# The last, half-filled chunk of four FFN down products: three full-height matmuls per output become one full-height and one half-height

## The reference, cut to what matters

```
def swiglu(h, w1, w3, w2):
    return (jax.nn.silu(h @ w1) * (h @ w3)) @ w2      # D_MODEL = 1024, D_FF = 2752, SEQ = 256

x = x + 0.5 * m[:, 0, 2][:, None] * swiglu(adaln_in(x, norm_g[l, 0], m, 0), ...)
```

## Time and profile before

| | |
|---|---|
| median of 3 executions | 1446.82 us |
| the profiled execution's own time | 1446.1 us |
| its span | 1444.3 us |
| PE busy | 1373.6 us, 95% of the span, 10822 matmuls |
| PE weight loads busy | 1309.9 us, 91% |
| DVE busy | 1088.4 us, 75% |
| ACT busy | 692.9 us, 48% |
| mean granted TensorE clock | 0.99 |

### The profile page before, as it was taken

The page is one execution under the profiler, slowest core; times in us unless marked ns, Lnnn a source line. Parts: engine busy times, 40 slices in busy tenths (PEclk is TensorE's granted clock), DMA queues, the critical chain, the costliest instruction groups (busy, mean ns, idle before and its releaser), DMA issues.

```text
span 1444.3 us, 26188 instructions
## 1 busy us (share of the span) xinstructions
PE 1373.6 (95%) x10822; PEld 1309.9 (91%) x10822; DVE 1088.4 (75%) x1832; ACT 692.9 (48%) x1121; POOL 24.9 (2%) x24
## 2 busy tenths in 40 slices
PE   2899999899999999999998999999999899999998
PEld 2899998789999989999997799999997678899998
DVE  6788998887787789788678766565676766677766
ACT  3343435554433363334464444344476866555453
POOL 0000000000000000001000000000010120000000
PEclk9999999999999999999999999999999999999999
DMA  9897758246868576584643145655422314154451
GB/s 392 345 403 310 312 198 315 95 189 261 309 263 319 207 284 267 215 346 192 250 184 124 59 175 205 230 199 214 175 89 102 117 62 185 64 201 175 179 192 69
DMA packets 32182, 305.80 MB, mean 212 GB/s; under 512 B 3480, under 2 KB 5784, under 8 KB 7360
## 3 DMA queue, kind: packets, MB, share of 16 engines
q1 hardware_dynamic: 32064, 304.13, 54.5%
HBM read 303.05 MB, written 1.06 MB: 211 GB/s over the span
## 4 chain that ended last, share of the span: by engine, by line
PE 83%; DVE 8%; DMA 4%; ACT 3%; issue 2%; SPq 0%; DVEq 0%; ACTq 0%
PE bank L692 13%; PE bank L696 13%; PE bank L693 13%; PE bank L867 12%; PE bank L786 7%; PE bank L784 7%; PE bank L791 6%; DMA ring<-in_stream 3%; PE bank L661 2%; DVE WL L1842 2%; PE bank L710 1%; DMA PR<-in_stream 1%; ACT WH L1285 1%; PE bank L768 1%; PE bank L960 1%
## 5 line engine op out<-in xcount | busy, mean ns | idle before, releaser
L1842 DVE TENSOR_TENSOR WL<-ring,WH 128x1024 fp32r<-128x1024 f32 x414 | 495.9, 1222 | 56.1 <-ACT WH L1285 54.0
L1285 ACT ACTIVATE WH<-ring 128x1024 fp32r<-128x1024 f32 x414 | 424.6, 1054 | 152.2 <-DMA ring<-in_stream 57.7
L692 PE MATMUL bank<-XH,WH 128*128 128x256 f32 x1648 | 403.0, 283 | 4.1 <-ACT WH L1285 4.1
L693 PE MATMUL bank<-XL,WH 128*128 128x256 f32 x1648 | 401.1, 282 | 0.0
L692 PEld LDWEIGHTS bank<-XH,WH 128*128 128x128 f32 x1648 | 311.1, 189 | 10.2 <-issue 9.0
L693 PEld LDWEIGHTS bank<-XL,WH 128*128 128x128 f32 x1648 | 311.2, 189 | 0.5 <-issue 0.5
L696 PE MATMUL bank<-XH,WL 128*128 128x256 f32 x1648 | 229.4, 282 | 0.0
L696 PEld LDWEIGHTS bank<-XH,WL 128*128 128x128 f32 x1648 | 209.9, 188 | 0.1
L784 PE MATMUL bank<-GH,WH 128*128 128x256 f32 x840 | 202.6, 279 | 0.1
L786 PE MATMUL bank<-GL,WH 128*128 128x256 f32 x840 | 202.5, 279 | 0.0
L1368 ACT ACTIVATE SG<-bank 128x256 f32<-128x256 f32 x84 | 32.2, 384 | 333.9 <-PE bank L696 328.9
(11 more groups left out here) (315 smaller groups left out, 1575.6 us busy)
## 6 DMA issues: line engine op xcount, KB each, us to landing
ring<-in_stream SPq DMA_DIRECT2D x128, 1536.0 KB, 6.6
scr<-in_stream SPq DMA_DIRECT2D x15, 1536.0 KB, 10.8
PR<-in_stream SPq DMA_DIRECT2D x15, 1536.0 KB, 9.5
att<-in_stream SPq DMA_DIRECT2D x15, 1536.0 KB, 10.3
ring<-in_stream SPq DMA_DIRECT2D x13, 1024.0 KB, 4.9
ring<-in_stream SPq DMA_DIRECT2D x10, 512.0 KB, 3.7
kf_mix<-in_stream SPq DMA_DIRECT2D x2, 1536.0 KB, 17.0
con<-in_consts SPq DMA_DIRECT2D x1, 1680.0 KB, 14.7
```

The source lines that it names most:

```text
L692: pe.matmul(o, part(WH, u, k), XH[:, k, :], start=(k == 0), stop=False)
L693: pe.matmul(o, part(WH, u, k), XL[:, k, :], start=False, stop=False)
L1285: act.activation(part_all(WH, u), raw(u), ACT.Copy).then_inc(*mark("high", u))
L1842: dve.tensor_tensor(part_all(WL, u), raw(u), part_all(WH, u).bitcast(F32), ALU.subtract)\
```

## The change

For the half chunk, three things differ. (1) VectorE writes the low part of the w2 unit not into WL but over the zero rows 0..63 of its WH slot. (2) VectorE makes a second copy of the rounded G32, into rows 0..63 of GH. (3) TensorE makes, per output m, one product of the full height, which now holds WH·GH in its lower 64 rows and WL·GH in its upper 64 rows, and one product of rows 64..127 alone, WH·GL. The left-over L763 of chunk 20 stays as it is.

```
                             if m == KD - 1:
                                 before.then_inc(*mark("ffn_down", f, c - 1))
-                            for w, x in ((WH, GH), (WH, GL), (WL, GH)):
-                                last = pe.matmul(out(m), part(w, u, m), x[:, c % 2, :], start=False, stop=(w is WL),
-                                                 skip_group_check=True)
-                            last.then_inc(*mark("ffn_out", f, m))
+                            pe.matmul(out(m), part(WH, u, m), GH[:, c % 2, :], start=False, stop=False, skip_group_check=True)
+                            pe.matmul(out(m), part(WH, u, m)[64:P], GL[64:P, c % 2, :], start=False, stop=True,
+                                      skip_group_check=True).then_inc(*mark("ffn_out", f, m))
...
                         dve.wait_ge(*at("high", u))
-                        dve.tensor_tensor(part_all(WL, u), raw(u), part_all(WH, u).bitcast(F32), ALU.subtract)\
-                            .then_inc(*mark("low_dve", u))
+                        name = UNITS[u][0]
+                        if name[0] == "w2" and half_chunk(name[1], name[2]):
+                            low, h = part_all(WH, u)[0:64], slice(64, P)
+                        else:
+                            low, h = part_all(WL, u), slice(0, P)
+                        dve.tensor_tensor(low, raw(u)[h], part_all(WH, u)[h].bitcast(F32), ALU.subtract).then_inc(*mark("low_dve", u))
...
                     if c >= 2:
                         dve.wait_ge(*at("ffn_down", f, c - 2))
+                    if half_chunk(f, c):
+                        dve.tensor_copy(GH[0:64, c % 2, :], G32[h])
                     link(dve.tensor_copy(GH[h, c % 2, :], G32[h]))
```

## The result

The changed kernel takes 1477.83 us (median of 4 runs, 1476.96 to 1479.05); the kernel before takes 1447.95 us (4 runs). The ratio is 1.0211, 95% interval [1.0197, 1.0226]. The forecast was 1459.1 us, with a range up to 1463.5: right about slower, wrong about how much. The profiled execution took 1477.21 us with a span of 1475.3, 31.0 us over the span before.

The account below looks back on a forecast made before the run. TensorE was taken to bound the kernel, VectorE arriving last at all four FFN ends. Per FFN -0.94 + 3.15 + 0.30, written +9.9 in all on 1446.8 us, plus 2.4 for the clock: 1459.1 us, range 1453.5 to 1463.5.

Parts of the forecast that it names:

- What bounds the kernel: TensorE's time counts in full at the FFN ends, VectorE arrives last at all four; DMA is 4% of the path.
- The product that goes: At each FFN end, 24 matmuls in place of 32: 0.94 us less on TensorE.
- The changes of form: Switching between full-height and 64-row products, 16 times per FFN end: 0.19 to 0.20 us each, 3.15 us per FFN.
- Rival (b): At the FFN ends, switching between full-height and 64-row fp32r products into one bank costs nothing: 1444.2 us; chance 0.06.
- (c): Rival: at the FFN ends only one switching direction costs, or half of each, 1.6 us per FFN: 1450.7 us; chance 0.06.
- VectorE's copy: Second copy into GH, on the chain TensorE waits for at all four FFN ends: 0.30 us each, 1.2 in all.
- The low part's new place: VectorE's low part of the w2 unit, 64 rows in place of 128: no change in time, cost 0.
- The clock: TensorE's clock falls to 1.2 GHz once behind each of the first two FFN ends: 1.2 us each, 2.4 together.
- The bounds: For the whole kernel's time, a range of 1453.5 to 1463.5 us around the forecast of 1459.1.
- a fall at all four ends: Rival: TensorE's clock falls in full behind all four FFN ends, 4 x 1.75 us: 1463.7 us; four or more, chance 0.08.
- one to three falls: The forecast's own case, TensorE's clock falling at one to three FFN ends: 1457.9 to 1461.5 us; chance 0.58.

Follow-up runs that it names:

- e1: Changed kernel with the GL product at full height again, GpSimd zeroing GL rows 0..63, no half-height product: 1448.71 us, ratio 0.9993 to the kernel before.
- e3: Kernel before, still three products for the half chunk, but WH x GL made of rows 64..127 alone and no second copy: 1469.74 us.
- e9: Changed kernel with TensorE's wait for VectorE ahead of the four tails filled by 18, 15, 10 and 4 unused full-height products: 1468.83 us.
- e5: Changed kernel with two full products and then two half products per pair of outputs, 8 changes of form per FFN end: 1461.36 us.
- e11: Kernel before with 55 unused full-height products behind each of the four tails, no change of form: 1474.20 us, ratio 1.0195.
- e6: Changed kernel with two unused full-height products per output between the full and the half product: 1479.36 us.
- e2: Kernel before with only VectorE's second copy into GH added: 1450.94 us, ratio 1.0021.
- e4: Changed kernel with the eight half products behind the sixteen full ones, two changes of form per FFN end: 1450.58 us.
- e10: Changed kernel with two unused full-height products per output, and TensorE's wait for VectorE ahead of each tail filled too: 1467.58 us.

## Why the prediction was wrong, step by step

- **What bounds the kernel: right.** VectorE is last ahead of every tail, PE's time in the tail arrives in full at the end of the sums, and no DMA took anything up.
- **The product that goes, 0.94 us: right** (e1: 3.85 to 2.80 to 2.91).
- **The changes of form: right.** I read 0.19 to 0.20 each off and took 3.15 us per end; e3 measured 3.00 and 3.04 with nothing else changed. In the changed kernel the tail at the high clock is 5.86 to 5.94 (e9), 6.0 forecast. Rival (b), that fp32r into one bank would escape it, is out, and so is (c), which had 1.6 us per FFN for the sixteen where e3 has 3.0. Each change costs the same within the error: eight cost half of sixteen (e5, 4.35 - 2.91 = 1.44).
- **VectorE's copy: right, 0.28. The low part's new place: wrong.** I had it at nothing, since its duration would stay 1.22. It did, but in this place VectorE's instructions started 0.08 to 0.09 ahead of the end of the one before, and on either side of the new one they start 0.03 to 0.04 behind it (rows below). That is 0.25 us where VectorE sets PE's start: the two together 2.0 us in place of 1.2.
- **The clock: the step that failed.** I wrote that it would fall "once behind each of the first two, and not behind the other two", for 1.2 us each, 2.4 in all. It fell at all four ends, for 10.2, 10.2, 6.7 and 6.7 us. The ends and the sums grew by 23.8 us; at the high clock they would have grown by 4 x ((5.90 + 3.56) - 7.30) = 8.6 us, so that the clock took 15.2 there, where I had 2.4. Elsewhere the changed kernel's profile has 5.2 us more at the low clock, of which the 4.6 of the third layer are mostly not the change's (e11). Three things were wrong. I read the length of a low stretch off the one window of the earlier trace rows and priced it at 3.5 us. The trace behind that window, the line below, has a mean of 0.55, which is (1 - 0.55) / 0.50 x 3.5 = 3.15 us more, and the earlier trace rows shows the slow products in it. So even that stretch lasted about 6.8 us and was worth up to 3.4, not 1.75. Next, among changes of form it can last longer still: 13.7 us in e6 and e3, against 3.5 in e2. And I thought that the wait ahead was needed, which e9 and the fourth end deny. What was measured without the clock's term is 8.6 + 2.0 = 10.6 us, where my sum had 9.9.

```profile
792.00:795.50 3.50, 3.50 (x20) 3.44 (x19) 2.92 (x9) 2.44 (x10) 0.00 (x0) 0.55 0.00 0
```

- **The bounds.** I priced a fall at all four ends at 4 x 1.75 and gave it 0.08. The range ended at 1463.5 since I had no row of a low stretch inside a tail with changes of form, and put the end at the nearest one instead of asking how long it could last. Four falls of 3.4 us would have been 13.6, and 1470.3. The upper bound of 1461.5 for one to three falls doesn't come out of the prices either: three at 1.2 make 1460.3, and 1461.5 is four.

VectorE's rows for the low part, ahead of the third tail of the changed kernel:

```profile
735.83 1.22 DVE L1846 TENSOR_TENSOR WL<-ring,WH 128x1024 fp32r<-128x1024 f32 x1
737.08 1.22 DVE L1846 TENSOR_TENSOR WH<-ring,WH 64x1024 fp32r<-64x1024 f32 x1
738.34 1.29 DVE L1901 CUSTOM_DVE_ANT_0 att<-att,cond,par 128x1024 f32<-128x1024 f32 x1
```

The same three instructions in the kernel before, all of 128 rows:

```profile
721.25 2.35 DVE L1842 TENSOR_TENSOR WL<-ring,WH 128x1024 fp32r<-128x1024 f32 x2
723.52 1.28 DVE L1898 CUSTOM_DVE_ANT_0 att<-att,cond,par 128x1024 f32<-128x1024 f32 x1
```

From the first start to the third it was 2.27 us and is 2.51: 0.12 at each of the two starts. That it is the 64 rows isn't shown: elsewhere in the kernel before, VectorE starts a full-height instruction 0.08 us ahead of the end of a copy of 64 rows (the L2085 of the earlier trace rows, which ends at 253.94):

```profile
253.86 1.21 DVE L1842 TENSOR_TENSOR WL<-ring,WH 128x1024 fp32r<-128x1024 f32 x1
```

What stays open is which part of a thin tail the clock reacts to: why e3 kept it at its first end, behind a wait of 1.5 us, and lost it at the third, behind 0.5, no run here explains. Nor does a run thin the tail in another way, with idle time and no change of form, so that the thinness and the changes aren't told apart as what the clock reacts to. What is shown is that the low clock grows with their number: the third and fourth end kept the high clock with two and with eight changes (e4, e5) and lost it with sixteen in the changed kernel.

## What to carry to other kernels

Count the changes of form before you count matmuls: a 64-row product between full ones costs 0.19 us going in and 0.19 coming out here, over three times the 0.118 that a full product takes. Where zeros can stand in the unused rows, pay the full height. And price a thinner TensorE stream for its clock as well as for its gaps: at the four ends the clock took 15 us, more than the 12 (64 x 0.19) of the changes of form themselves, and 8 of the 15 it took in the dense sums behind the tails.

## What the runs showed of the hardware that I had not expected

- A kernel with 111 more matmuls was 10 us faster (e10 against the changed kernel), since the clock stayed at 2.4 GHz at the four ends.
- In the thirteen tails with eight or sixteen changes of form in which the clock fell, it rose only 1.9 to 5.6 us behind the last change, after 3.4 to 13.7 us. In e1 and e2, without changes of form, it rose inside the tail, after 3.4 to 3.5.
- The third layer, which no edit touches, took 395.0 to 401.8 us in the thirteen profiles, with 10 to 27 us of low clock in it. A few us between two single profiles are no effect of an edit there.
- Single runs of e6 lie 8 us apart (1471.04, 1479.35, 1479.38, 1487.34), with about 41, 62, 59 and 83 us of low clock: the low stretch at an end seems to come or stay away from run to run.
